# The recurrence's last two inverse levels cut to their nonzero blocks, its steps in a new order, and its modulation formed on GpSimd and ScalarE in the first dense stage

## The reference

```
mod = c @ ada_w + ada_b                  # 6 x 1024: shift, scale, gate (twice)
h   = rmsnorm(x) * (1 + mod[scale]) + mod[shift]
z   = h @ w_in                           # r, k, v, lora parts, zu, zv
y1  = gelu(zu) * (W_s @ layernorm(zv))   # gMLP mixer, W_s causal over the tokens
y2  = RWKV-7 mixer                       # state S_t = S_(t-1)(diag(w) - a b^T) + v k^T
x   = x + mod[gate] * ([y1, y2] @ w_out) ; then a mixture of experts on it, with mod 3 to 5
```

## Time and profile before

| what | value |
|---|---|
| median of 3 runs | 2396.05 us (2395.46 to 2401.61) |
| profiled execution, span | 2395.9 us |
| TensorE busy | 2264.7 us (95%) |
| VectorE busy | 1237.3 us (52%) |
| ScalarE busy | 808.8 us (34%) |
| GpSimd busy | 380.6 us (16%) |
| the last dense unit (zu) ends on TensorE | 187.4 us |
| chunk 1 starts / chunk 3 starts | 217.43 / 284.49 us |

### The profile page before, as it was taken

How to read it: one execution, slowest core, us unless ns; L and a number is a source line. 1 busy time by engine, 2 the same in 40 slices (tenths; PEclk the granted TensorE clock), 3 DMA queues, 4 the chain that set the end, 5 groups by cost and what they waited for, 6 DMA issues and landing times.

```text
span 2395.9 us, 34312 instructions
## 1 busy us (share of the span) xinstructions
PE 2264.7 (95%) x14568; PEld 1645.9 (69%) x14568; DVE 1237.3 (52%) x1625; ACT 808.8 (34%) x1201; POOL 380.6 (16%) x265
## 2 busy tenths in 40 slices
PE   8999998997789989999999999999999999999998
PEld 5677885322223327877677699899787668989976
DVE  5885654300000007365765498486463749938745
ACT  3533232111011105123452354243342836514424
POOL 1001001100001000000000154252100024605310
PEclk9999999999999999999999999999999999999999
DMA  7223316999999993222111123333222012233330
GB/s 297 72 87 120 125 71 281 397 420 420 419 417 420 420 383 157 89 96 80 36 56 68 55 96 102 105 104 107 112 89 87 1 53 80 95 108 106 108 112 36
DMA packets 59020, 388.76 MB, mean 162 GB/s; under 512 B 7739, under 2 KB 7867, under 8 KB 17008
## 3 DMA queue, kind: packets, MB, share of 16 engines
q1 hardware_dynamic: 52896, 375.29, 40.9%
q0 software_dynamic: 5104, 8.09, 0.9%
q10 hardware_dynamic: 864, 3.15, 0.4%
HBM read 383.13 MB, written 13.63 MB: 166 GB/s over the span
## 4 chain that ended last, share of the span: by engine, by line
PE 79%; DMA 10%; DVE 5%; ACT 3%; SPq 1%; issue 1%; POOL 0%; DVEq 0%; POOLq 0%; ACTq 0%
PE psD L3570 38%; PE psD L2656 8%; PE psA L2656 8%; DMA ring<-w_moe 8%; PE psD L1424 7%; PE psA L3570 3%; DMA arena<-w_moe 1%; PE psA L1424 1%; SPq L804 1%; PE psA L2640 1%; DVE ring_r L3169 1%; PE psA L3645 1%; ACT ring_r L2951 1%; PE psA L3862 1%; PE psA L3802 1%
## 5 line engine op out<-in xcount | busy, mean ns | idle before, releaser
L3570 PE MATMUL psD<-rounded,ring_r 128*128 128x512 f32 (+1 forms) x3192 | 759.3, 398 | 6.8 <-DVE ring_r L3169 3.3
L3570 PEld LDWEIGHTS psD<-rounded,ring_r 128*128 128x128 f32 (+1 forms) x3192 | 594.6, 187 | 166.9 <-issue 16.5
L1424 PE MATMUL psD<-ring,arena 128*32 128x512 f32 x1568 | 177.2, 594 | 30.7 <-DMA ring<-w_moe 30.2
L3169 DVE TENSOR_TENSOR ring_r<-ring,ring_r 128x2048 fp32r<-128x2048 f32 (+2 forms) x71 | 158.9, 2238 | 81.7 <-ACT ring_r L2951 79.7
L2656 PE MATMUL psD<-rounded,fast_r 128*128 128x256 f32 x1680 | 200.0, 279 | 0.0
L2656 PE MATMUL psA<-rounded,fast_r 128*128 128x256 f32 x1680 | 199.8, 279 | 0.0
L1424 PE MATMUL psD<-arena 128*32 128x512 f32 x1504 | 173.5, 602 | 27.1 <-DMA arena<-w_moe 25.0
L2656 PEld LDWEIGHTS psA<-rounded,fast_r 128*128 128x128 f32 x1680 | 198.2, 188 | 0.4
L2656 PEld LDWEIGHTS psD<-rounded,fast_r 128*128 128x128 f32 x1680 | 198.1, 188 | 0.1
L2951 ACT ACTIVATE ring_r<-ring 128x2048 fp32r<-128x2048 f32 (+2 forms) x71 | 131.8, 1856 | 192.6 <-PE psD L3570 172.7
L3570 PE MATMUL psD<-rounded,fast_r 128*128 128x512 f32 x792 | 185.4, 395 | 0.0
(11 more groups left out here) (552 smaller groups left out, 2738.5 us busy)
## 6 DMA issues: line engine op xcount, KB each, us to landing
ring<-w_dense SPq DMA_DIRECT2D x134, 1024.0 KB, 4.9
ring<-w_moe SPq DMA_DIRECT2D x49, 2048.0 KB, 34.0
arena<-w_moe SPq DMA_DIRECT2D x47, 2048.0 KB, 33.4
ring<-w_dense SPq DMA_DIRECT2D x16, 768.0 KB, 4.2
ring<-w_dense SPq DMA_DIRECT2D x16, 640.0 KB, 3.9
arena<-pair_rows SPq DMA_DIRECT2D x8, 512.0 KB, 8.0
arena<-x_t SPq DMA_DIRECT2D x1, 2048.0 KB, 8.0
token_rows<-arena ACTq DMA_DIRECT2D x4, 512.0 KB, 11.0
```

The source lines that it names most:

```text
L1424: mm = pe.matmul(bank_[32 * g:32 * g + 32], rows(g), weights(g), start=start, stop=stop_)
L3169: dve.tensor_tensor(lo_, src, hi, ALU.subtract).then_inc(sem("w_lo"), 1)
L3570: mm = pe.matmul(out, w[a], x[b], start=start and i == 0, stop=stop_ and i == 2)
```

## The change

1. Slices 8 to 23 of `ada_w` are stored transposed (outputs on the partitions, the 1024 inputs in a row) and loaded among the units of the first dense stage. GpSimd multiplies each by c (`times_c`, two tensor_tensors per slice, 128x2x896 and 128x2x128). ScalarE adds up the products with two Copy activations of 128x1024 with an accumulator (`modulation`). The slots are released by ScalarE. TensorE's products with c (16 of them) and the row-to-column steps in the recurrence are gone; VectorE adds `ada_b` once, at the end.
2. Levels 5 and 6 multiply only the blocks that aren't zero: 32x32 blocks at level 5, 64x64 at level 6. Copies shrink with them, and the level masks and GpSimd's refills are gone.
3. In a chunk the steps stand in another order: half of `ak` comes before sa and half after it, level 5 begins after st, the mixer's `mix_tokens` comes after `whole_5`; VectorE takes the blocks of chunk d+1 ahead of `scales` of chunk d-1. PSUM banks are planned anew (`aux_plan`).

```diff
-        mat(("ada", j), "ada_w", 0, cols(256 * j, 256 * j + 256))
+        unit(("ada", j), KT, 256, lambda a, j=j: np.asarray(a["ada_w"][0])[:, 256 * j:256 * j + 256].T
+             .reshape(2, P, D).transpose(1, 0, 2))
...
-LOAD_ORDER = [*range(4), FIRST_K, *range(4, FIRST_K), *range(FIRST_K + 1, len(PLAN))]
+ADA = {j: UNITS_OF[("ada", j)][0][0] for j in range(24)}
+MORE_ADA = {ADA[j]: j for j in range(8, 24)}
+FIRST_LOADS = [("ada", 0), ("ada", 1), ("ada", 2), ("ada", 3), ("k", 0), ("ada", 4), ("ada", 5), ("ada", 6), ("ada", 7),
+               ("k", 1), ("lora_wa",), ("r", 0), ("ada", 8), ("r", 1), ("ada", 9), ("v", 0), ("ada", 10), ("v", 1),
+               ("ada", 11), ("lora_g",), ("ada", 12), ("zv",), ("ada", 13), ("zv",), ("ada", 14), ("zu", 0), ("ada", 15),
+               ("zu", 1)]
+FIRST_LOADS += [("ada", j) for j in range(16, 24)] + [("w_out", j) for j in range(4)]
+_seen = {}
+LOAD_ORDER = []
+for _g in FIRST_LOADS:
+    LOAD_ORDER.append(UNITS_OF[_g][_seen.get(_g, 0)][0])
+    _seen[_g] = _seen.get(_g, 0) + 1
+assert sorted(LOAD_ORDER) == list(range(N_FIRST))
+LOAD_ORDER += range(N_FIRST, len(PLAN))
...
+    a += [("vt", 0), ("bt", 0)] + four("ab", 0) + four("ak", 0) + [("gm", MIX_ORDER[0]), ("kt", 0)]
+    a += [("u", 0, 5), ("xt", 0, 5), ("u", 0, 6), ("xt", 0, 6)]
     for d in range(1, NCH):
-        a += four("ab", d) + four("ak", d) + [("gm", MIX_ORDER[d])] + tokens(d) + [("gnm", d - 1)]
-        a += two("u", d, 5) + [("mr", d + 1, 0), ("mr", d + 1, 1), ("gnv", d - 1)] + two("xt", d, 5)
-        a += [("mo", d, 0), ("mr", d + 1, 2)] + two("u", d, 6) + [("mr", d + 1, 3)]
-        a += two("xt", d, 6) + [("gns", d - 1), ("gg", d - 1), ("mo", d, 1)]
+        a += four("ab", d) + four("ak", d) + [("u", d, 5)] + tokens(d) + [("gnm", d - 1), ("xt", d, 5), ("gm", MIX_ORDER[d])]
+        a += [("u", d, 6), ("gnv", d - 1), ("xt", d, 6), ("gg", d - 1), ("gns", d - 1)]
...
+                    if before in MORE_ADA:
+                        modulated(sp_, MORE_ADA[before])
+                    elif before in SPLIT_NO:
                         sp_.wait_ge(sem("w_lo"), SPLIT_NO[before] + 1)
                     else:
...
+                if i == ADA[8]:
+                    sp_.wait_ge(sem("units_done"), FIRST_K + 1)
+                    for dst, lo, hi in C_ROW:
+                        sp_.dma_start(dst, w_dense[len(PLAN) + 2][:, lo:hi]).then_inc(sem("par_in"), 16)
+                if i == ADA[20]:
+                    sp_.wait_ge(sem("units_done"), last_unit(("zu", 0)) + 1)
+                    sp_.dma_start(ring[:, g2_at:g2_at + UNIT], w_dense[len(PLAN) + 1]).then_inc(sem("gm2_in"), 16)
+                if i == ADA[21]:
+                    sp_.wait_ge(sem("units_done"), last_unit(("zu", 1)) + 1)
+                    sp_.dma_start(ring[:, g1_at:g1_at + UNIT], w_dense[len(PLAN)]).then_inc(sem("gm1_in"), 16)
...
+            def times_c(*units):
+                for j in units:
+                    u, nk, nco = UNITS_OF[("ada", j)][0]
+                    w = ring_of(u, nk, nco).rearrange("p k n -> p (k n)").rearrange("p (a n) -> p a n", a=2)
+                    loaded(pool, u)
+                    for row, lo, hi in C_ROW:
+                        step(pool.tensor_tensor(w[:, :, lo:hi], w[:, :, lo:hi], bc(row, [P, 2, hi - lo], 1), ALU.mult))
+                    pool.nop().then_inc(sem("mod_mul"), 1)
+            pool.wait_ge(sem("par_in"), 64)
+            times_c(8, 9, 10, 11)
             pool.wait_ge(sem("ar"), 4)
             step(pool.memset(INV, 0.0))
             pool.memset(INV[:, 0:1024:33], 1.0).then_inc(sem("consts"), 1)
+            times_c(*range(12, 22))
             group_ready(pool, ("zu", 1))
...
+            times_c(22, 23)
+            pool.wait_ge(sem("gm2_in"), 16)
+            heads_map(HEADS2)
+            step(pool.tensor_tensor(HEADS2, HEADS2, G2[:, 2, :], ALU.mult))
+            pool.nop().then_inc(sem("ws_causal"), 1)
...
+            def modulation(*units):
+                for j in units:
+                    u, nk, nco = UNITS_OF[("ada", j)][0]
+                    w = ring_of(u, nk, nco).rearrange("p k n -> p (k n)").rearrange("p (a n) -> p a n", a=2)
+                    act.wait_ge(sem("mod_mul"), j - 7)
+                    for i in range(2):
+                        ins = act.activation(w[:, i, :], w[:, i, :], ACT.Copy, accum_out=mod[:, 2 * j + i:2 * j + i + 1])
+                    ins.then_inc(sem("mod_done"), 1)
...
+            modulation(13, 14)
...
+            modulation(15, 16, 17)
             root(small[:, 48:52])
+            modulation(18, 19, 20, 21)
             group_ready(act, ("zu", 1))
...
+            def halfway_5(d):
+                n_ = ("u", d, 5)
+                ready(act, n_)
+                act.activation(UI[5], bank(n_)[:, 0:256], ACT.Copy).then_inc(freed(n_), 1)
+            def halfway_6(d):
+                n_ = ("u", d, 6)
+                ready(act, n_)
+                act.activation(UI[6][64:P], bank(n_)[64:P], ACT.Copy).then_inc(freed(n_), 1)
...
             def level_5(d):
+                n_ = ("xt", d, 5)
+                ready(dve, n_)
+                v = bank(n_)[:, 0:256].rearrange("p (h t) -> p h t", h=8)
+                xi = XI.rearrange("p (h t) -> p h t", h=8)
+                xt = XTS[d % 2].rearrange("p (h t) -> p h t", h=8)
+                step(dve.transpose(xi[32:64, :, 0:32], v[0:32]))
+                dve.nop().then_inc(sem("x_new"), 1)
+                step(dve.tensor_copy(xt[64:96, :, 96:P], v[64:96]))
+                take(n_, dve.tensor_copy(xt[0:32, :, 32:64], v[0:32]))
...
+            diagonals(0)
             for d in range(NCH):
-                diagonals(d)
                 ab_masks(d)
                 ak_masks(d)
-                mixed(MIX_ORDER[d])
-                if d > 0:
+                if d == 0:
+                    mixed(MIX_ORDER[0])
+                else:
                     new_state(d - 1)
                     centred(d - 1)
+                level_5(d)
+                if d > 0:
+                    mixed(MIX_ORDER[d])
+                if d > 0:
                     asked_at = variance(d - 1)
-                    scales(d - 1, asked_at)
-                level_5(d)
-                columns(d, 0)
                 if d == NCH - 1:
                     yc_lo(0, CONV_P[1], YC[:, 0:4, :], CONV_P[0])
                 level_6(d)
-                if d == NCH - 1:
+                if d + 1 < NCH:
+                    diagonals(d + 1)
+                else:
                     ahead(last_unit(("w_out", 0)))
                 if d > 0:
+                    scales(d - 1, asked_at)
                     normed(d - 1)
-                columns(d, 1)
+            dve.wait_ge(sem("mod_done"), 16)
+            step(dve.tensor_tensor(mod[:, 16:48], mod[:, 16:48], pc("ada_b", 16, 32), ALU.add))
...
+            def half_5(d):
+                pe.wait_ge(sem("lm"), d + 2)
+                out = aux(("u", d, 5))
+                xi = XI.rearrange("p (h t) -> p h t", h=8)
+                for h in range(8):
+                    for lo in (0, 64):
+                        mm = pe.matmul(out[lo + 32:lo + 64, 32 * h:32 * h + 32], LM[lo:lo + 32, h, lo + 32:lo + 64],
+                                       xi[lo:lo + 32, h, lo:lo + 32], start=True, stop=True)
+                filled(mm)
...
+            def half_6(d):
+                out = aux(("u", d, 6))
+                pe.wait_ge(sem("x_new"), 2 * d + 1)
+                xi = XI.rearrange("p (h t) -> p h t", h=8)
+                for h in range(8):
+                    mm = pe.matmul(out[64:P, 64 * h:64 * h + 64], LM[0:64, h, 64:P], xi[0:64, h, 0:64],
+                                   start=True, stop=True)
+                filled(mm)
...
             for d in range(1, NCH):
                 products("ab", A, d)
                 u0(d - 1)
+                products("ak", K, d, (0,))
                 sa(d - 1)
-                products("ak", K, d)
+                products("ak", K, d, (2,))
                 y(d - 1)
-                mix_tokens(MIX_ORDER[d])
                 st(d - 1)
+                half_5(d)
                 by_tokens(d)
                 group_mean(d - 1)
-                half(5, d)
-                modulation(d + 1, 0, 8 + 4 * d)
-                modulation(d + 1, 1, 9 + 4 * d)
+                whole_5(d)
+                mix_tokens(MIX_ORDER[d])
+                half_6(d)
                 group_squares(d - 1)
-                whole(5, d)
-                to_column(("mo", d, 0), MROW, 4, ("mr", d + 1, 1))
-                modulation(d + 1, 2, 10 + 4 * d)
-                half(6, d)
-                modulation(d + 1, 3, 11 + 4 * d)
-                whole(6, d)
-                group_scales(d - 1)
-                to_column(("mo", d, 1), MROW, 4, ("mr", d + 1, 3))
+                whole_6(d)
+                group_scales(d - 1, gate_first=True)
```

216 lines of the change are left out of this document (72 added, 144 removed).

## The result

The changed kernel takes 2424.11 us in the median of 4 runs (2422.56 to 2430.2), the kernel before 2398.52 us (4 runs); the ratio is 1.0105, with a 95% interval of 1.0092 to 1.0118. The change makes the kernel 25.6 us, or 1%, slower. The profiled execution has a span of 2422.6 us against 2395.9.

A forecast was written before the change was run, and what follows sets the result against it. It took TensorE to hold most of the chain, with VectorE close behind in the first stage. First stage and chunk 0 +39.5 and recurrence -16 gave +23.5 on 2395.9, that is 2419 us, range 2378 to 2440.

The forecast's parts named there:

- the time up to chunk 1: First dense stage and chunk 0: GpSimd's slices delay VectorE, so chunk 1 begins at 257, +39.5 us.
- the last chunk: End of the recurrence: 3 us saved in VectorE's chain, 0.7 at the head by half of `ak` ahead of sa.
- The exclusion and the alternation: First dense stage: GpSimd's products and VectorE's two-SBUF-input operations can't overlap and take turns; last cut 28.4 us late; chance 0.60.
- From the normalisation to chunk 1: Normalisation ends at 223.2, second `ab` pair stands 39.3 us late; chunk 0 counted even, so chunk 1 is 39.5 late.
- Loads cost nothing by this count: Slice loads: a slot is refilled during another unit's product, so loads add no time.
- the heavier rival: Recurrence gains only 6 us and the lower clock in chunk 0 adds 10: 2440 us, chance 0.05.
- The recurrence's price: Chunks: 9.8 us of TensorE work goes, 3.7 comes back, 6.1 stays; two periods make 12.2, -16 in all.
- The small blocks: Levels 5 and 6 in a chunk: 96 records at 0.044 us each, hence 4.2 us.
- the removed slices show in full: Each chunk: four slices of 1.07 us leave TensorE, 4.3 us, counted as saved time.
- The returned wait for the norm: Chunks: `scales` behind level 6 and the next chunk's transposes gives back about 2.2 us with the semaphores.
- No price for the port: First stage: GpSimd slips into times when VectorE reads PSUM, has one input or waits: 2380 us, chance 0.20.
- VectorE keeps the port: First stage: short waits let GpSimd not in, slices 15 to 21 start after `substitute`, +20: 2400 us, chance 0.15.

The follow-up runs named there:

- experiment 1: Changed kernel with GpSimd's multiplications by c left out, waits and ScalarE's sums kept: 2390.56 us, ratio 0.9963 to the kernel before.
- experiment 2: Changed kernel with each slice's two GpSimd multiplications replaced by three memsets into the same slot: 2400.67 us, ratio 1.0010.
- Experiment 7: Changed kernel with slices 11 to 23 loaded, multiplied and summed in the recurrence: 2397.26 us, ratio 0.9979.
- experiment 12: Kernel before with each of the sixteen modulation slices in the recurrence formed by one 128x256 product instead of eight: 2398.05 us, ratio 0.9988.
- Experiment 4: Changed kernel with `scales` put ahead of level 6 and of the next chunk's transposes in VectorE's order: 2424.13 us, ratio 1.0099.
- experiment 3: Changed kernel with slices 15 to 23 multiplied after VectorE's normalisation, in the recurrence: 2393.71 us, ratio 0.9983.
- experiment 5: Changed kernel with each slice's two GpSimd products cut in nine pieces of at most 256 columns: 2424.11 us, ratio 1.0101.
- experiment 6: Changed kernel with slices 12 to 21 multiplied by VectorE instead of GpSimd: 2410.88 us, ratio 1.0041.
- experiment 9: Changed kernel with idle products on TensorE in the waits for the norm: 2416.92 us, ratio 1.0076.

## Why the prediction was right, and where it wasn't

The forecast was 2419 (+23.5); it is 2424 (+25.6). Its mechanism, the exclusion in the first stage, holds. That the number is so near is luck: the time up to chunk 1 was forecast 8.9 us too dear and the last chunk 12.0 too cheap, and the two nearly cancel.

- **The exclusion and the alternation: right.** One operation of VectorE gets in between two of GpSimd. The rows after show it, experiment 1 removes it, and experiment 2 shows that GpSimd's time by itself doesn't hold VectorE up. Experiment 7 has the same exclusion in the recurrence. A slice was priced at 4.8 us and takes 4.0 + 0.8. Slices 15 to 18 stood at 166.8 to 188.5, predicted 167.6 to 190.2. The last cut came 24.6 us late (28.4 predicted), the normalisation ended at 222.3 (223.2). The rule of the Trainium skill, "SBUF — State Buffer", section "SBUF: two separate sides", that the shared port pair is an exclusive lock between operations of VectorE with two SBUF inputs and operations of GpSimd that read SBUF, agrees with all of these, and the memsets, which read nothing, fit it.
- **From the normalisation to chunk 1: mis-sized.** "Loads cost nothing by this count" didn't hold: slice 19, and with it 20 and 21, waited for a slot that the late cut freed (16.16 us on GpSimd). I had slices 19 and 20 beside the normalisation and slice 21 behind it, its sum done at 230.5; in fact three slices ran beside it from 204.67 on, and the sum was done at 223.3. The block copies ended at 228.1 instead of 235.4. Chunk 0 then took 4.71 us of wait for the sums of slices 22 and 23. Chunk 1 was 30.6 us late, 39.5 predicted. The clock in chunk 0 was counted in the heavier rival alone; it was at the lower level for about 12 of the 18.7 us from 229.34 on.
- **The recurrence's price: right in sum, not in its parts.** Two periods gave back 11.4 us, 12.2 predicted. The small blocks are 2 x 0.69 + 2 x 1.14 = 3.7 us for 4.2 predicted. But that the removed slices show in full, 4.3 us a chunk, isn't borne out by experiment 12: in the kernel before, 1.0 of 2.8 us shows in chunk 2 and nothing in chunk 1. The returned wait for the norm was counted at 2.2 and is 2.36 us. It took 1.36 us for four transposes; the row has three (all four are 1.84 us), and the changed kernel has three too, so the term came out. Experiment 4 shows that the place of `scales` isn't to blame.
- **The last chunk: wrong sign.** I counted -3.7. It cost +8.3, since the wait for the norm is 4.97 us there and the clock fell for 20 us behind the wait of chunk 2 and for 10 us behind this one. The step that failed is that a returned wait costs its own length: a pause of 2.4 us brought up to 20 us of work at 1.2 GHz. No case of the prediction had this cost; its rival of 0.05 has the slow clock in chunk 0 only. The size is that of one trace, though. Where the lower level lasted 7 us (experiments 1, 2, 3, 5 and 6), the last stretch cost +1.9: still no gain, and 6.4 us less than here.
- **The rivals.** "No price for the port" would have been 2380; with the multiplications out the kernel takes 2390.6. "VectorE keeps the port" didn't happen: there are gaps between its operations where they wait on one another, and GpSimd got in at the next one each time.

Open: what the small blocks and the new order give apart from each other. Neither was undone as a whole.

Also open: how much of the lateness goes when ScalarE does the gelu of zu ahead of the sums of slices 18 to 21. No experiment has this order.

The best version is the changed kernel with the slices from 11 or 15 on multiplied in the recurrence and the waits filled (ratios 0.9975 and 0.9976), 0.24% faster than the kernel before and 1.3% faster than the change. Without the filling it is 0.9979 and 0.9983; the intervals overlap, so between these four nothing is decided.

## What to carry to other kernels

Before work is given to an idle GpSimd, look at what VectorE does in the same stretch: beside operations with two SBUF inputs a product of 4.8 us on GpSimd took 4.1 us from VectorE, which would need 2.45 us for it. Operations that read PSUM aren't held up. But there, too, a single operation with two SBUF inputs that TensorE waits for is enough (3.92 instead of 0.69 us in experiment 7), and so are the sums on ScalarE ahead of a copy. And work taken off TensorE counts only as far as TensorE doesn't wait there already; a new pause of 2 us has to be priced with the clock behind it, here 7 to 20 us at the lower level.

## What the runs showed of the hardware

- A memset of GpSimd (1.8 us for 2048 columns) held up none of VectorE's two-input operations, but a TENSOR_SCALAR went from 0.55 to 1.01 us and another from 0.17 to 1.08.
- TensorE's clock fell to its lower level behind pauses of 2.4 us, and stayed there for different lengths: 7 us behind the wait at the end of chunk 1 and 20 behind the same wait at the end of chunk 2 of the changed kernel, but 7 behind the latter in experiments 1, 3 and 5. Shorter pauses did it too, or didn't: 14 us at the lower level (272 to 285) came behind a pause of 0.89 us in experiment 4, none behind 1.16 us in experiment 9.
- Cutting GpSimd's products in pieces of 256 columns cost VectorE 3.7 us a slice, while the two whole products took 4.1 us from it.
